# First norm inside the setup, and modulation's weight tiles of 4096 columns with three of them in front of the scan

## Chip, cores and metric

The kernel runs on one core of a Trainium2 chip. The metric is the device time of one execution in microseconds; the kernel before takes 2419.62 us (median of 3 runs, 2417.17 to 2423.88).

## What is computed

Two transformer blocks over 256 tokens of width 1024, in float32. What the change touches is the first block's first norm, its projection and S5 branch, and the second block's modulation, which needs only `c`, `c_ctx` and `ada_w` and is computed early, beside the first block:

```python
h = rms_norm(x, norm_mix_pre[l])                 # y * rsqrt(mean(x*x) + 1e-6) * gain
proj = h @ w_in[l]                               # 1024 x 4096: q, k, v, u, gate_logits
...
lam_bar = exp(lam * dt)                          # S5 branch: 32 groups, 64 complex states each
_, states = associative_scan(combine, (decay, bu), axis=1)
y = einsum('gcp,bsgp->bsgc', c_mat, states).real + d_skip * ug
y = gelu(y); o_ssm = y * sigmoid(y @ w_glu + b_glu)
...
merged = gate_attn * (o_attn @ w_branch_attn[l]) + gate_ssm * (o_ssm @ w_branch_ssm[l])
...
def ada_params(cond, w, b):                      # second block, for c and c_ctx, two layers
    m = silu(cond) @ w + b                       # w: 1024 x 6144
    return split(m, 6)
```

## The kernel before, in words

Activations are kept with features on the partitions: `xT` and `hT` are [128, 8 chunks, 256 tokens]. All weights pass through a ring of four slots of 2 MB (`K.ring`, [128, 4096] each). `K.queue` (116) fixes at build time which weight tile goes to which slot; `K.issue` (138) is the program of SyncE in each stage: it issues the next tiles in this order, and waits before each until the products that read the slot's previous tile are done (`K.done_at`). The queue in order is: 8 tiles of `w_in`, 16 of `ada_w`, `ssm_w_glu` (1 MB), 8 of `ada_w`, `w_branch_attn`, `w_branch_ssm`, `w_out`, and so on. A tile of `ada_w` holds 512 columns of all 1024 rows (`rows_of`), so every partition reads eight runs of 2 KB.

Each stage is a block with one program per engine, and a block begins when all engines have left the one before. The stages here:

- `stage_setup` (203): SyncE loads x, half of the parameter vectors and then issues four tiles; ScalarE issues the other half; TensorE turns x and the parameter rows by transposes, and VectorE copies them to `xT` and `params`.
- `stage_norm` (378): ScalarE squares `xT`, TensorE sums over the partitions with `ones`, ScalarE takes the root, VectorE the reciprocal and `hT = xT * gain * rstd`.
- `linear_stage` (532), the projection: 8 tiles of 4 chunks. `ssm_params` (781) runs beside it: GpSimd loads five small tensors and scales them, and TensorE turns them in `first_turns` (805), between the first and the second tile; VectorE works out the scan's tables.
- `stage_ssm_scan` (989): 16 steps. TensorE makes the drive two steps ahead (`make_drive`), then does one ada tile, then reads out the states (four products at line 1033); VectorE rotates and scans, GpSimd rotates back. ScalarE spreads the decay (1096), and after step 1 does `ada_conditions` (silu of c and c_ctx); TensorE's first ada tile waits for that.
- `stage_glu`, then `stage_stick_breaking` (592): attention in 4 pairs of heads; an ada tile before pairs 0 and 1, one in each pair, two behind the last. `stage_merge` (1128) needs both branch weights.

An ada tile is 8 products of one row chunk against 512 columns (`ada_beside`, 1475). The stationary operand is `c`, [128, 8, 62], zero but for columns 30 and 31; its slice `30 - 2i` puts the two results of tile i into rows 2i and 2i + 1 of a PSUM group of 32. Four groups work side by side, each on two of the eight row chunks. `move` copies this to SBUF and `turn` sums the four parts while turning it.

Of the kernel before, what the change touches and what calls it, by code (L numbers as in the profile page):

```python
# [18 lines left out]
ACT = mybir.ActivationFunctionType  # L19
# [29 lines left out]
ADA_SCAN = 16  # L49
# [153 lines left out]
def stage_setup(K):  # L203
# [25 lines left out]
    turned, moved = K.counter("rows_turned"), K.counter("rows_moved")  # L229
    with K.stage() as st:  # L230
        table = K.sb("param_rows", [P, n_tiles, P], ctx=st)
        x_rows = K.sb("x_rows", [P, TT, D], ctx=st)
        ps = K.ps("setup_ps", [P, 2, 512], st)
        block = st.enter_context(nc.Block())
        n_sync = len(pieces) // 2

        @block.sync
        def _(sp):
            sp.dma_start(x_rows[:, :, :], io["x"][0].rearrange("(a p) d -> p a d", p=P)).then_inc(x_loads.sem, x_loads.tick())
            for t, r, n, a in pieces[:n_sync]:  # L240
                if t == n_tiles - 1:
                    sp.wait_ge(made.sem, made.at(1))
                sp.dma_start(table[r:r + n, t, :], a).then_inc(loads.sem, loads.tick())
            K.issue(sp, 0)

        @block.scalar
        def _(act):
            act.wait_ge(made.sem, made.at(1))
            for t, r, n, a in pieces[n_sync:]:
                act.dma_start(table[r:r + n, t, :], a).then_inc(loads.sem, loads.tick())  # L250

# [18 lines left out]
        @block.tensor  # L270
        def _(pe):
            pe.wait_ge(made.sem, made.at(5))
            pe.wait_ge(x_loads.sem, x_loads.at(1))
            for q in range(quads + -(-n_tiles // 4)):
                if q >= 2:
                    pe.wait_ge(moved.sem, moved.at(q - 1))
                if q == quads:
                    pe.wait_ge(loads.sem, loads.at(len(pieces)))
                n = 4 if q < quads else min(4, n_tiles - 4 * (q - quads))
                for j in range(n):  # L280
                    if q < quads:
                        a, c = divmod(4 * q + j, KC)
                        src = x_rows[:, a, c * P:(c + 1) * P]
                    else:
                        src = table[:, 4 * (q - quads) + j, :]
                    mm = pe.transpose(ps[:, q % 2, j * P:(j + 1) * P], src, K.ident[:, :])
                mm.then_inc(turned.sem, turned.tick())

        @block.vector
        def _(dve):  # L290
            for q in range(quads + -(-n_tiles // 4)):
                dve.wait_ge(turned.sem, turned.at(q + 1))
# [6 lines left out]
                dve.tensor_copy(dst, ps[:, q % 2, 0:n * P].rearrange("p (a n) -> p a n", n=P)).then_inc(moved.sem, moved.tick())  # L299

# [291 lines left out]
def stage_stick_breaking(K, qT, kT, v, oT):  # L592
# [9 lines left out]
    with K.stage() as st:  # L602
# [17 lines left out]
        def _(pe):  # L620
# [33 lines left out]
            for i in range(pairs):  # L654
                sum_later(i)
                if i + 2 < pairs:
                    make_scores(i + 2)
                ada_multiply(pe, i + 2)
                mix(i)
            for n in range(pairs + 2, ada_tiles):  # L660
                ada_multiply(pe, n)
            ada_turn(pe)
# [50 lines left out]
        def _(dve):  # L713
# [33 lines left out]
            ada_move(dve, lambda out, x: dve.tensor_copy(out, x))  # L747
# [241 lines left out]
def stage_ssm_scan(K, S, uT, yT):  # L989
# [4 lines left out]
    with K.stage() as st:  # L994
# [12 lines left out]
        def _(pe):  # L1007
# [10 lines left out]
            make_drive(1)  # L1018
            for i in range(ST):
                if i + 2 < ST:  # L1020
                    make_drive(i + 2)
                if i == 0:
                    pe.wait_ge(silued.sem, silued.at(2))
                    pe.wait_ge(cleared.sem, cleared.at(2))
                ada_multiply(pe, i)
# [10 lines left out]
            ada_turn(pe)  # L1036
# [55 lines left out]
        def _(act):  # L1092
            for i in range(ST):
# [3 lines left out]
                if i == 1:  # L1097
                    ada_conditions(K, None, act)
            ada_move(act, lambda out, x: act.activation(out, x, ACT.Copy))
# [277 lines left out]
def queue_first_block(K):  # L1377
    io = K.io
    queue_columns(K, io["w_in"][0], 4096)
    ada = [(l, c) for l in range(2) for c in range(0, 6 * D, 512)]  # L1380
    for l, c in ada[:ADA_SCAN]:
        K.queue((0, (KC, 512), rows_of(io["ada_w_2"][l], c, 512)))
    queue_columns(K, io["ssm_w_glu"][0], 512)
    for l, c in ada[ADA_SCAN:]:
        K.queue((0, (KC, 512), rows_of(io["ada_w_2"][l], c, 512)))
# [13 lines left out]
def first_block(K):  # L1399
    gain = lambda name: (lambda c: K.col(name, c))  # L1400
    with ExitStack() as K.part:
# [4 lines left out]
        with ExitStack() as banks:  # L1406
            with ExitStack() as ssm:
# [3 lines left out]
                stage_norm(K, K.xT, K.hT, gain("norm_mix_pre"))  # L1411
# [55 lines left out]
def ada_setup(K):  # L1467

    K.ada = {"row": K.sb("ada_row", [P, 512], ctx=K.part), "c": K.sb("ada_c", [P, KC, 62], ctx=K.part),
             "parts": K.sb("ada_parts", [P, 32], ctx=K.part)}


def ada_beside(K, first, n):
# [8 lines left out]
    def multiply(pe, i):  # L1484

        w = K.tile(pe, g0 + i, KC)
        for k in range(2):
            for part in range(4):
                mm = pe.matmul(ps[32 * part:32 * part + 32, :], c[:, 2 * part + k, 30 - 2 * i:62 - 2 * i], w[:, 2 * part + k, :],
                               start=i == 0 and k == 0, stop=i == n - 1 and k == 1, tile_position=(0, 32 * part),  # L1490
                               skip_group_check=True)
        mm.then_inc(full.sem, full.tick())
        K.done_at[g0 + i] = full.count

    def turn(pe):

        pe.wait_ge(free.sem, free.at(1))
        for j in range(4):
            pe.matmul(tiles[:, first:first + n, j, :], row[:, j * P:(j + 1) * P], parts[:, 0:2 * n], start=True, stop=True)

    def move(eng, copy):

        eng.wait_ge(full.sem, K.done_at[g0 + n - 1])
# [1657 lines left out]
```

## Time and profile before

| | us |
|---|---|
| median of 3 runs | 2419.62 |
| the profiled execution's own time | 2414.2 |
| its span | 2412.4 |
| TensorE busy with products | 2161.8 (90%) |
| VectorE, ScalarE, GpSimd busy | 610.2, 440.1, 224.8 |
| DMA | 575.46 MB, 239 GB/s over the span |

Times in the rows are microseconds from the span's start. "PE" is TensorE's products, "PEld" its weight loads, "DVE" VectorE, "ACT" ScalarE, "POOL" GpSimd, "SP" SyncE, and a q behind a name is the engine's queue of issues. A float32 product appears as two records. "idle before <- X" is how long the engine had been idle and whose work ended it. The profile's clock is the share of 2.4 GHz that was granted to TensorE; 0.5 is 1.2 GHz. A stretch's mean lies between.

### The profile page before, as it was taken

How to read it: one execution, taken by the hardware profiler on the slowest of the kernel's cores; microseconds unless marked ns; L12 is line 12 of the kernel's file. 1: busy time of each engine (PE TensorE's matmuls, PEld its weight loads, DVE VectorE, ACT ScalarE, POOL GpSimd, SP SyncE). 2: the span in 40 equal slices, each digit the busy share in tenths (PEclk: the TensorE clock that was granted, in tenths of full speed). 3: DMA queues.
4: the chain of work that ended last, by engine and by line, in shares of the span. 5: the costliest groups of instructions: out<-in, count | busy, mean ns of one | idle time of the engine just before them, and what ended most of it. 6: DMA issues, size and time to landing. Idle time of an engine off the chain costs nothing. (4 is left out here: it accounts for less than half of the span.)

```text
span 2412.4 us, 25196 instructions
## 1 busy us (share of the span) xinstructions
PE 2161.8 (90%) x10420; PEld 1393.5 (58%) x10420; DVE 610.2 (25%) x1387; ACT 440.1 (18%) x835; POOL 224.8 (9%) x352
## 2 busy tenths in 40 slices
PE   6989799779999898889988999898879899988887
PEld 5754486668878755577767433333358754333334
DVE  3557221122210324753223111111012221111111
ACT  1221311112211325533322000000011210000001
POOL 2024100001010114100000100000000000000000
PEclk8999999989999799989888999999989899999998
DMA  6469933224432121210037999999944679999994
GB/s 205 140 224 387 365 140 116 94 87 140 150 137 87 35 70 35 70 36 1 1 119 291 407 428 427 427 427 428 420 172 148 244 326 428 427 428 428 427 428 192
DMA packets 123662, 575.46 MB, mean 239 GB/s; under 512 B 5216, under 2 KB 28345, under 8 KB 99481
## 3 DMA queue, kind: packets, MB, share of 16 engines
q1 hardware_dynamic: 122079, 570.59, 59.5%
q10 hardware_dynamic: 970, 2.23, 0.3%
q8 instruction: 87, 1.43, 0.2%
q0 software_dynamic: 496, 0.97, 0.2%
q14 instruction: 30, 0.25, 0.0%
HBM read 572.72 MB, written 1.05 MB: 238 GB/s over the span
## 5 line engine op out<-in xcount | busy, mean ns | idle before, releaser
L567 PE MATMUL linear_ps<-hT,ring 128*128 128x256 f32 x1216 | 267.2, 382 | 14.4 <-PEq L384 12.4
L2749 PE MATMUL ex_u<-ring_extra,ex_xt 128*64 128x512 f32 x1024 | 235.2, 614 | 36.9 <-DMA ring_extra<-in_w 36.9
L567 PEld LDWEIGHTS linear_ps<-hT,ring 128*128 128x128 f32 x1216 | 232.6, 192 | 48.8 <-issue 16.9
L2749 PE MATMUL ex_u<-ring,ex_xt 128*64 128x512 f32 x1024 | 230.3, 604 | 28.5 <-DMA ring<-in_w 27.0
L2749 PEld LDWEIGHTS ex_u<-ring_extra,ex_xt 128*64 128x64 f32 x1024 | 81.8, 141 | 188.2 <-issue 188.2
L2749 PEld LDWEIGHTS ex_u<-ring,ex_xt 128*64 128x64 f32 x1024 | 81.3, 139 | 173.9 <-issue 173.9
L1831 PE MATMUL dl_front<-dn_src,ring 128*128 128x256 f32 (+1 forms) x512 | 177.5, 503 | 2.4 <-DVE dp_cv L1998 2.4
L2854 DVE TENSOR_TENSOR ex_hid<-ex_sil,ex_u 128x512 f32<-128x512 f32 x32 | 34.8, 1088 | 496.2 <-PE ex_u L2749 496.2
L1279 PE MATMUL ffn_ps<-hT,ring 128*128 128x256 f32 x704 | 154.9, 384 | 5.9 <-PEq L442 5.9
L1279 PEld LDWEIGHTS ffn_ps<-hT,ring 128*128 128x128 f32 x704 | 135.6, 193 | 25.2 <-issue 6.3
L1831 PEld LDWEIGHTS dl_front<-dn_src,ring 128*128 128x128 f32 x512 | 100.0, 200 | 65.6 <-issue 57.9
L2722 PE MATMUL ex_yT<-ex_back,ex_ys 128*128 128x256 f32 x512 | 124.2, 385 | 3.0 <-DVE ex_ys L2865 1.6
L2787 PE MATMUL ex_u<-ring_extra,ex_hidT 128*64 128x512 f32 x512 | 113.8, 596 | 1.0 <-ACT ex_hidT L2811 1.0
L2722 PEld LDWEIGHTS ex_yT<-ex_back,ex_ys 128*128 128x128 f32 x512 | 92.2, 190 | 37.5 <-issue 21.1
L2787 PE MATMUL ex_u<-ring,ex_hidT 128*64 128x512 f32 x512 | 113.4, 595 | 0.0
L2688 POOL COPY ex_xt<-hT 128x256 f32 x60 | 24.1, 402 | 742.2 <-PE ex_u L2749 580.3
L2865 DVE COPY ex_ys<-ex_u 128x512 f32<-128x512 f32 x32 | 22.1, 692 | 239.1 <-PE ex_u L2787 239.1
L1347 PE MATMUL down_ps<-ffn_hid,ring 128*128 128x256 f32 x352 | 78.0, 384 | 4.6 <-PEq L1264 4.6
L2807 ACT ACTIVATE ex_sil<-ex_u 128x512 f32<-128x512 f32 x32 | 19.1, 597 | 318.0 <-PE ex_u L2749 318.0
L1347 PEld LDWEIGHTS down_ps<-ffn_hid,ring 128*128 128x128 f32 x352 | 67.8, 193 | 14.4 <-issue 5.0
L2787 PEld LDWEIGHTS ex_u<-ring_extra,ex_hidT 128*64 128x64 f32 x512 | 35.2, 137 | 69.6 <-issue 68.1
L2787 PEld LDWEIGHTS ex_u<-ring,ex_hidT 128*64 128x64 f32 x512 | 35.3, 137 | 69.3 <-issue 69.3
(549 smaller groups left out, 2511.1 us busy)
## 6 DMA issues: line engine op xcount, KB each, us to landing
ring<-in_w SPq DMA_DIRECT2D x96, 2048.0 KB, 25.3
ring_extra<-in_w SPq DMA_DIRECT2D x92, 2048.0 KB, 25.7
ring<-in_ada_w SPq DMA_DIRECT2D x24, 2048.0 KB, 13.2
ring<-in_ffn_w_up SPq DMA_DIRECT2D x22, 1024.0 KB, 6.5
ring<-in_w_in SPq DMA_DIRECT2D x8, 2048.0 KB, 8.7
ring<-in_w_in_a SPq DMA_DIRECT2D x8, 2048.0 KB, 8.5
ring<-in_w_in_b SPq DMA_DIRECT2D x6, 2048.0 KB, 18.5
ring<-in_ffn_w_down SPq DMA_DIRECT2D x5, 2048.0 KB, 8.1
```

The costliest lines, as they stand in the source:

```text
L567: mm = pe.matmul(ps[:, q % banks, 0:n], w[:, k, j * P:(j + 1) * P], src[:, k, 0:n], start=k == 0, stop=k == kc - 1)
L1279: mm = pe.matmul(ps[:, c % 4, j * T:(j + 1) * T], w[:, j * KC + k, (c % per) * P:(c % per + 1) * P], src[:, k, :], start=k == 0, stop=k == ...
L1347: mm = pe.matmul(ps[:, c // 2, c % 2, :], w[:, f % per, c * P:(c + 1) * P], hid[:, f, :], start=f == 0 and c % 2 == 0, stop=f == FC - 1 an ...
L1831: mm = pe.matmul(ps[:, h % 2, 0:segs * T], w[:, i, (h % 4) * P:(h % 4 + 1) * P], src[:, i, 0:segs * T], start=i == 0, stop=i == KC - 1)
L2688: ins = pool.tensor_copy(xt[:, p % 2, 4 * i:4 * i + 4, H * a:H * a + H], part[:, :, bass.ds(start, H)])
L2722: mm = pe.matmul(yT[:, c // 2, c % 2, :], ys[:, p % 2, c * P:(c + 1) * P], back[:, p % 2, :], start=p == 0 and c % 2 == 0, stop=p == pairs ...
L2749: mm = pe.matmul(u[H * a:H * a + H, i, :], xt[:, b, k, H * a:H * a + H], w[a][:, 512 * k:512 * k + 512], start=k == 0, stop=k == KC - 1, s ...
L2787: mm = pe.matmul(u[H * a:H * a + H, n, :], hidT[:, k, H * a:H * a + H], cols, start=k == 0, stop=k == fc - 1, skip_group_check=True)
L2807: act.activation(sil[:, :], u[:, 0, :], ACT.Silu).then_inc(silued.sem, silued.tick())
L2854: dve.tensor_tensor(hid[:, :].rearrange("s (k q) -> s k q", k=fc), sil[:, :].rearrange("s (q k) -> s k q", k=fc), u[:, 1, :].rearrange("s ...
L2865: dve.tensor_copy(ys[:, p % 2, 512:1024], u[:, 1, :]).then_inc(y1_moved.sem, y1_moved.tick())
```

## The change

Three parts. First, the norm's stage is gone. The setup now squares x while the tokens are on the partitions (ScalarE, the sum over a token's features from the accumulator), takes root and reciprocal on two columns, scales the rows (`n_rows`, half by VectorE, half by ScalarE), turns them by sixteen more transposes, and multiplies by the gain on the way from PSUM to `hT`. SyncE issues two weight tiles in the setup instead of four; the other two go out at the projection's start. Second, an ada tile is now either one row chunk against its first 4096 columns (one run of 16 KB per partition), or, each third, the last 2048 columns of two row chunks (two DMAs with runs of 8 KB). Each layer is 12 tiles as before, but all of a layer has to be there before its results can be moved. Third, 18 instead of 16 tiles are done in the scan's stage, three of them in front of its first step, none in its last; six instead of eight are left for the attention. Layer 0 is moved and turned inside the scan. ScalarE does the conditions before its first spread.

```diff
-ADA_SCAN = 16
+ADA_SCAN = 18
+ADA_FRONT = 3
...
-            K.issue(sp, 0)
+            K.issue(sp, 0, until=2)
+
+        all_moved = TT * KC // 4 + -(-n_tiles // 4)
 
         @block.scalar
         def _(act):
             act.wait_ge(made.sem, made.at(1))
             for t, r, n, a in pieces[n_sync:]:
                 act.dma_start(table[r:r + n, t, :], a).then_inc(loads.sem, loads.tick())
+            act.wait_ge(made.sem, made.at(4))
+            act.activation(root[:, TT:TT + 1], K.epsb[:, :], ACT.Sqrt)
+            act.wait_ge(x_loads.sem, x_loads.at(1))
+            for t in range(TT):
+                act.activation(n_rows[:, t, :], x_rows[:, t, :], ACT.Square, scale=D ** -0.5,
+                               accum_out=root[:, t:t + 1]).then_inc(squared.sem, squared.tick())
+            act.wait_ge(squared.sem, squared.at(TT))
+            act.activation(root[:, 0:TT], root[:, 0:TT], ACT.Sqrt, bias=K.epsb[:, :]).then_inc(rooted.sem, rooted.tick())
+            act.wait_ge(inverted.sem, inverted.at(1))
+            act.activation(n_rows[:, 1, :], x_rows[:, 1, :], ACT.Copy, scale=root[:, 1:2]).then_inc(scaled.sem, scaled.tick())
+            act.wait_ge(moved.sem, moved.at(all_moved))
+            for c in (2, 3, 6, 7):
+                act.wait_ge(chunked.sem, chunked.at(c // 2 + 1))
+                act.activation(K.hT[:, c, :], n_ps[:, c // 2, c % 2, :], ACT.Copy, scale=gain(c))
...
+            pe.wait_ge(scaled.sem, scaled.at(2))
+            for c in range(KC):
+                for t in range(TT):
+                    mm = pe.transpose(n_ps[:, c // 2, c % 2, t * P:(t + 1) * P], n_rows[:, t, c * P:(c + 1) * P], K.ident[:, :])
+                if c % 2:
+                    mm.then_inc(chunked.sem, chunked.tick())
...
+                if q == quads:
+                    dve.wait_ge(rooted.sem, rooted.at(1))
+                    dve.reciprocal(root[:, 0:TT], root[:, 0:TT]).then_inc(inverted.sem, inverted.tick())
+                    dve.wait_ge(inverted.sem, inverted.at(1))
+                    dve.tensor_scalar(n_rows[:, 0, :], x_rows[:, 0, :], root[:, 0:1], None, ALU.mult).then_inc(scaled.sem, scaled.tick())
...
+            dve.wait_ge(moved.sem, moved.at(all_moved))
+            for c in (0, 1, 4, 5):
+                dve.wait_ge(chunked.sem, chunked.at(c // 2 + 1))
+                dve.tensor_scalar(K.hT[:, c, :], n_ps[:, c // 2, c % 2, :], gain(c), None, ALU.mult)
...
-                ada_multiply(pe, i + 2)
+                if i + 2 < ada_tiles:
+                    ada_multiply(pe, i + 2)
                 mix(i)
             for n in range(pairs + 2, ada_tiles):
                 ada_multiply(pe, n)
-            ada_turn(pe)
+            ada_turn(pe, 1)
...
+            pe.wait_ge(silued.sem, silued.at(2))
+            pe.wait_ge(cleared.sem, cleared.at(2))
+            for n in range(ADA_FRONT):
+                ada_multiply(pe, n)
             for i in range(ST):
                 if i + 2 < ST:
                     make_drive(i + 2)
-                if i == 0:
-                    pe.wait_ge(silued.sem, silued.at(2))
-                    pe.wait_ge(cleared.sem, cleared.at(2))
-                ada_multiply(pe, i)
+                if i + ADA_FRONT < ADA_SCAN:
+                    ada_multiply(pe, i + ADA_FRONT)
+                if i + ADA_FRONT == ADA + 1:
+                    ada_turn(pe, 0)
...
+            ada_conditions(K, None, act)
             for i in range(ST):
                 if i >= 2:
                     act.wait_ge(scanned.sem, scanned.at(i - 1))
                 act.activation(rr[:, i % 2, :], S["cos"][:, i, :], ACT.Identity, scale=0.0, bias=S["r"][:, i:i + 1]).then_inc(spread.sem, spread.tick())
-                if i == 1:
-                    ada_conditions(K, None, act)
-            ada_move(act, lambda out, x: act.activation(out, x, ACT.Copy))
+                if i + ADA_FRONT == ADA:
+                    ada_move(act, 0, lambda out, x: act.activation(out, x, ACT.Copy))
...
-                stage_norm(K, K.xT, K.hT, gain("norm_mix_pre"))
...
+def ada_products(t):
+
+
+
+    q, kind = divmod(t, 3)
+    if kind < 2:
+        return [(2 * q + kind, j, 512 * j) for j in range(8)]
+    return [(2 * q + h, 8 + j, 2048 * h + 512 * j) for h in range(2) for j in range(4)]
+
+
+def queue_ada(K, g):
+
+    l, t = divmod(g, ADA)
+    q, kind = divmod(t, 3)
+    w = lambda k, c, n: K.io["ada_w_2"][l, k * P:(k + 1) * P, c:c + n]
+    if kind < 2:
+        K.queue((0, (1, SLOT), w(2 * q + kind, 0, SLOT)))
+    else:
+        K.queue(*((2048 * h, (1, 2048), w(2 * q + h, SLOT, 2048)) for h in range(2)))
...
-        w = K.tile(pe, g0 + i, KC)
-        for k in range(2):
-            for part in range(4):
-                mm = pe.matmul(ps[32 * part:32 * part + 32, :], c[:, 2 * part + k, 30 - 2 * i:62 - 2 * i], w[:, 2 * part + k, :],
-                               start=i == 0 and k == 0, stop=i == n - 1 and k == 1, tile_position=(0, 32 * part),
-                               skip_group_check=True)
+        l, t = divmod(first + i, ADA)
+        g = g0 + i
+        pe.wait_ge(K.landed[K.slot[g]], K.need[g])
+        w = K.ring[K.slot[g]]
+        if l and t == 0:
+            pe.wait_ge(free.sem, free.at(1))
+        for m, (k, j, at) in enumerate(ada_products(t)):
+            part = j % 4
+            mm = pe.matmul(ps[32 * part:32 * part + 32, :], c[:, k, 30 - 2 * j:62 - 2 * j], w[:, at:at + 512],
+                           start=t == 0 and m < 4, stop=t == ADA - 1 and m >= 4, tile_position=(0, 32 * part), skip_group_check=True)
         mm.then_inc(full.sem, full.tick())
-        K.done_at[g0 + i] = full.count
-
-    def turn(pe):
+        K.done_at[g] = full.count
```

## Rows read from the trace of the kernel before

**Rows 1.** Timeline, first 35 us: start, us, engine, line, operation, idle before.

```profile
6.06 3.48 PE L286 MATMUL setup_ps<-ident,x_rows 128*128 128x128 f32 x16 [6.06 <-DMA x_rows<-in_x]
...
7.14 0.27 ACTq L250 DMA_DIRECT2D param_rows<-in_onorm_a  x1
...
12.03 0.91 PE L286 MATMUL setup_ps<-ident,param_rows 128*128 128x128 f32 x5 [2.48 <-DMA param_rows<-in_final_norm]
...
18.71 1.28 ACT L395 ACT_TABLE_LOAD   x1 [18.71 <-PEq L230]
...
20.01 2.00 ACT L395 ACTIVATE hT<-xT 128x1024 f32<-128x1024 f32 x2
...
33.20 15.61 PE L567 MATMUL linear_ps<-hT,ring 128*128 128x256 f32 x64 [5.91 <-PEq L384]
```

**Rows 2.** Timeline of SyncE's queue at 17 to 19 us.

```profile
13.12 5.18 SPq L151 DMA_DIRECT2D ring<-in_w_in  x1
```

**Rows 3.** Timeline of TensorE in the scan.

```profile
150.88 1.92 PE L1489 MATMUL ada_ps<-ring,ada_c 128*32 128x512 f32 x16 [1.42 <-ACT ada_c L1521]
...
156.81 3.62 PE L1033 MATMUL ssm_yp<-ssm_pz,ssm_cT 128*32 128x256 f32 x8 [4.00 <-POOL ssm_pz L1089]
...
170.56 1.89 PE L1033 MATMUL ssm_yp<-ssm_pz,ssm_cT 128*32 128x256 f32 x8
...
175.19 1.89 PE L1033 MATMUL ssm_yp<-ssm_pz,ssm_cT 128*32 128x256 f32 x8
```

**Rows 4.** Stretches: length; PE, PEld, DVE, ACT, POOL busy (count); clock; DMA share; GB/s.

```profile
7.55:14.00 6.45, 2.90 (x16) 1.83 (x14) 3.20 (x6) 0.00 (x0) 0.00 (x0) 0.88 0.95 264
...
14.00:18.70 4.70, 0.00 (x0) 0.00 (x0) 0.00 (x0) 0.00 (x0) 0.00 (x0) 0.50 1.04 383
...
160.00:166.50 6.50, 6.50 (x25) 2.33 (x24) 4.03 (x6) 0.51 (x1) 2.27 (x3) 0.53 0.03 10
...
168.00:222.00 54.00, 54.00 (x331) 22.63 (x331) 51.12 (x72) 5.59 (x11) 29.81 (x22) 1.00 1.05 386
...
287.00:293.10 6.10, 6.09 (x16) 4.96 (x17) 0.00 (x0) 0.00 (x0) 0.00 (x0) 0.56 1.03 392
...
1400.00:1500.00 100.00, 97.94 (x456) 40.94 (x453) 12.37 (x28) 6.57 (x11) 6.01 (x16) 0.98 1.01 427
```

**Rows 5.** Timeline from the scan's end to the merge.

```profile
229.38 1.92 PE L1489 MATMUL ada_ps<-ring,ada_c 128*32 128x512 f32 x16 [1.37 <-DMA ring<-in_ada_w]
...
231.14 1.89 PE L1033 MATMUL ssm_yp<-ssm_pz,ssm_cT 128*32 128x256 f32 x8
...
233.28 1.33 ACT L1102 ACTIVATE ssm_y<-ssm_y 128x256 f32<-128x256 f32 x4
...
243.36 0.71 PE L626 MATMUL sb_z<-proj 64*128 64x256 f32 x4 [1.29 <-PEq L544]
...
276.43 3.64 PE L1489 MATMUL ada_ps<-ring,ada_c 128*32 128x512 f32 x32
...
280.88 1.07 PE L1499 MATMUL ada_t<-ada_parts,ada_row 128*128 128x16 f32 x8 [0.81 <-DVE ada_row L747]
...
287.01 3.75 PE L1147 MATMUL merge_ps<-o_attn,ring 128*128 128x256 f32 x8 [5.06 <-DMA ring<-in_w_branch_ssm]
```

**Rows 6.** Line 1249 (cross attention): the read of an accumulator; ns min/median/max.

```profile
L1249 ACT ACTIVATION_READ_ACCUMULATOR xa_p<-xa_s,xa_nm x8: 192/198/203, 451.0 to 475.0; 128x1 f32 x8
```

**Rows 7.** DMA issues at 7.6 and at 147.5 us: count, KB, us to landing.

```profile
ring<-in_w_in SPq DMA_DIRECT2D x1, 2048.0 KB, 9.0
...
ring<-in_ada_w SPq DMA_DIRECT2D x1, 2048.0 KB, 8.1
```

**Rows 8.** Timeline of the projection's first two tiles.

```profile
42.15 3.65 POOL L874 TENSOR_SCALAR ssm_cx<-ssm_cr,ssm_half 128x256 f32<-128x256 f32 x4
...
48.73 0.23 PE L807 MATMUL ssm_ps<-ident,ssm_ldr 16*128 16x16 f32 x1
...
49.82 13.98 PE L567 MATMUL linear_ps<-hT,ring 128*128 128x256 f32 x64
```

More of the change, by code:

```diff
@@ L229, in stage_setup @@
     turned, moved = K.counter("rows_turned"), K.counter("rows_moved")
+    squared, rooted, inverted, scaled, chunked = (K.counter(n) for n in (
+        "norm_squared", "norm_rooted", "hn_inverted", "norm_scaled", "rt_rowed"))
     with K.stage() as st:
@@ L232, in stage_setup @@
         x_rows = K.sb("x_rows", [P, TT, D], ctx=st)
+        n_rows = K.sb("x_normed", [P, TT, D], ctx=st)
+        root = K.sb("x_root", [P, TT + 1], ctx=st)
         ps = K.ps("setup_ps", [P, 2, 512], st)
+        n_ps = K.ps("setup_normed", [P, KC // 2, 2, T], st)
+        gain = lambda c: K.col("norm_mix_pre", c)
         block = st.enter_context(nc.Block())
@@ L746, in _ @@
                 store(i)
-            ada_move(dve, lambda out, x: dve.tensor_copy(out, x))
+            ada_move(dve, 1, lambda out, x: dve.tensor_copy(out, x))
         @block.sync
@@ L1035, in _ @@
                 mm.then_inc(y_full.sem, y_full.tick())
-            ada_turn(pe)
         @block.vector
@@ L1379, in queue_first_block @@
     queue_columns(K, io["w_in"][0], 4096)
-    ada = [(l, c) for l in range(2) for c in range(0, 6 * D, 512)]
-    for l, c in ada[:ADA_SCAN]:
-        K.queue((0, (KC, 512), rows_of(io["ada_w_2"][l], c, 512)))
+    for g in range(ADA_SCAN):
+        queue_ada(K, g)
     queue_columns(K, io["ssm_w_glu"][0], 512)
-    for l, c in ada[ADA_SCAN:]:
-        K.queue((0, (KC, 512), rows_of(io["ada_w_2"][l], c, 512)))
+    for g in range(ADA_SCAN, 2 * ADA):
+        queue_ada(K, g)
     for n in ("w_branch_attn", "w_branch_ssm"):
@@ L1484, in multiply, with turn, move @@
     def multiply(pe, i):
-        w = K.tile(pe, g0 + i, KC)
-        for k in range(2):
-            for part in range(4):
-                mm = pe.matmul(ps[32 * part:32 * part + 32, :], c[:, 2 * part + k, 30 - 2 * i:62 - 2 * i], w[:, 2 * part + k, :],
-                               start=i == 0 and k == 0, stop=i == n - 1 and k == 1, tile_position=(0, 32 * part),
-                               skip_group_check=True)
+        l, t = divmod(first + i, ADA)
[8 more added lines that the diff above has]
+                           start=t == 0 and m < 4, stop=t == ADA - 1 and m >= 4, tile_position=(0, 32 * part), skip_group_check=True)
         mm.then_inc(full.sem, full.tick())
-        K.done_at[g0 + i] = full.count
-    def turn(pe):
+        K.done_at[g] = full.count
+    def turn(pe, l):
         pe.wait_ge(free.sem, free.at(1))
         for j in range(4):
-            pe.matmul(tiles[:, first:first + n, j, :], row[:, j * P:(j + 1) * P], parts[:, 0:2 * n], start=True, stop=True)
-    def move(eng, copy):
-        eng.wait_ge(full.sem, K.done_at[g0 + n - 1])
+            pe.matmul(tiles[:, ADA * l:ADA * (l + 1), j, :], row[:, j * P:(j + 1) * P], parts[:, 0:2 * ADA], start=True, stop=True)
+    def move(eng, l, copy):
+        eng.wait_ge(full.sem, K.done_at[g0 + ADA * (l + 1) - 1 - first])
         copy(row[:, :], ps[:, :]).then_inc(free.sem, free.tick())
```

## Prediction

> **What bounds the kernel now.** I read three views in this order: the timeline of the first 35 us, the table of stretches, and the timeline from the scan to the merge. In the first 33 us TensorE has almost nothing to do: it turns x and the parameters and is done at 12.94, ScalarE starts the first norm at 18.71, and the first product of the projection starts at 33.20 [rows 1]. Between 13.7 and 18.71 no engine works; SyncE's queue is still inside the fourth 2 MB issue, which ends at 13.12 + 5.18 = 18.30 [rows 2], and the stage can't end before it. The projection then is TensorE's: 13.98 us for each weight tile at full clock, and nothing waits for DMA.
>
> From 148.3, where the projection ends, two things share the bound. In the scan TensorE has a drive product, an ada tile and a read-out per step, and a step takes 175.19 - 170.56 = 4.63 us [rows 3]; the transfers run without a gap at 386 GB/s from 168 to 222 [rows 4], 2.097 MB / 386 = 5.43 us a tile. So the queue is slower than TensorE, and only the three ada tiles that were loaded ahead hide it. The lead runs out at the end of the scan (1.37 us idle for an ada tile), and at 287.01 TensorE has sat 5.06 us for w_branch_ssm [rows 5]. What the queue lost stands in one row: from 160 to 166.5 it moved 10 GB/s while TensorE's clock was 0.53 [rows 4]. All four slots were full, and the step that frees one was slow because TensorE, idle for 4.00 us before 156.81, worked at its lower level of 1.2 GHz. After the merge TensorE is the bound again; each later stage is set by slots that earlier products free, so I let all behind 317.5 move as one piece. This costs nothing in my sum; the price if untrue is in the range.
>
> **Part 1: the norm in the setup.** Removed is everything from 18.71 to 33.20. Added to ScalarE behind its last parameter issue (7.14 + 0.28 = 7.42): a table load 1.28 and a one-column root, some 0.2 (8.90); two squares of 128x1024 at 1.00 with a read of the accumulator at 0.20 each (11.30); a root on two columns and a reciprocal, together about 0.6 with their semaphores (11.9); a copy of 128x1024 at 1.00 (12.9) [rows 1, 6]. VectorE scales the other half at the same time; the trace has no such instruction of that size, so I bound it by ScalarE's 1.00 from both sides, half of it and half as much again: it ends between 12.4 and 13.4. I take 13.0. VectorE's four xT copies are ahead of this and the parameter copies behind; the parameters have landed at 12.03, so TensorE turns them until 12.94 and VectorE's delayed copy is hidden behind TensorE's new turns. If it weren't, it would cost 0.9.
>
> Then sixteen more turns. The first sixteen took 3.48 us at full clock [rows 1]. But in the trace of before the clock is at 0.50 from 14.00 to 18.70 [rows 4], after a stretch in which TensorE had been idle for 2.48 us and then worked for 0.91. The new turns start there, so their bounds are 3.5 and 7.0 us; from 287.0 on, continuous work brought the clock back within 6.1 us [rows 4], so I take 5.2 in the middle: 18.2. The last two chunks are both ScalarE's, some 0.4 each by the linear stage's copies, and a change of block some 0.3: the projection starts at 19.3. Bounds 17.6 and 21.1. Its first weights landed at 7.55 + 9.0 = 16.6 [rows 7], earlier, so nothing waits for them. SyncE issues only two tiles in the setup and is free at 8.6, because the first two issues don't stall; tiles 2 and 3 go out when the projection starts and are needed 28 us later. Gain: 33.20 - 19.3 = 13.9. The first four chunks took 15.61 against 13.98 because of the low clock [rows 1, 8]; half of these 1.6 us may go: gain 0.8 (0 to 1.6).
>
> What moves with it: GpSimd's five SSM loads now start at 19.3, while tiles 1 to 3 are on the queue until 16.6 + 3 x 5.43 = 32.9. Before they had the queue for themselves; GpSimd's scalings ran from 42.15 for 3.65 us to 45.80, and TensorE asked for them at 48.73 [rows 8]. The slack is 2.9 us. If the loads land only with the last tile, at 32.9, GpSimd ends at 36.6 and TensorE, there at 34.8, waits 1.8; with their own packets behind that, 5. They are small and come in between, so I take 0.3 (bounds 0 and 5).
>
> Sum of part 1: 13.9 + 0.8 - 0.3 = 14.4 us. The projection itself is unchanged.
>
> **Part 2: tiles of 4096 columns.** The number of products a tile (8, in four groups side by side) and of bytes is the same, so TensorE's time stays: 1.92 us with the drain [rows 3], some 1.75 to the next product. What changes is the run of bytes: 2 KB per row before, 16 KB or 8 KB after. The experts' weights come in runs of 16 KB, and there the queue moves 427 GB/s, against 386 for ada [rows 4]: 4.91 us a tile. I take 427; bounds 386 and 427 (one in three tiles comes in 8 KB runs). The Trainium skill (DMA: Bandwidth & Descriptors, Specifications) puts line rate at 512 B and more, by which 2 KB rows gain nothing from being longer; the two rows speak against it, and by it the sum would be that of the first rival.
>
> **Part 3: three tiles in front.** Keep the clock of before in mind, with 148.3 as the end of the projection. ScalarE now does the conditions first, so the ada products can start at about 150.3 instead of 150.88 [rows 3]; its two rows for the scan come at 150.7, needed at 152.65, hidden. Three tiles take 5.3 us (155.6), then the third drive, about 1.1 (156.7), for which VectorE waits as long. Then ada tile 3 (landed: 147.5 + 8.1 = 155.6 [rows 7]) until 158.4, and the first read-out at 158.4 instead of 156.81. TensorE no longer sits 4.00 us there, so I keep its clock at full level; then the third read-out comes at 158.4 + 2 x 4.63 = 167.7 instead of 170.56. The slots are free at 152, 154 and 155.6, so the queue never stops: tile n has landed at 150.3 + 4.91 (n - 2), tile 17 at 224.0. TensorE by its own pace would be there at 156.7 + 14 x 4.63 = 221.5, so DMA sets the end: 224.0 + 1.75 + two read-outs of 1.8 = 229.4 against 231.14 + 1.89 = 233.03 before. Step 15 has no ada tile. If the clock did fall once more, TensorE would come 4.8 us late (10 us at about half) and the end only 2.3 late. The ada row's copy and turn move into the middle of the scan, where TensorE's 1.08 us are covered by the same 2.5 us of lead; at the end the table load no longer precedes the four gelus [rows 5], gain 0.7.
>
> Attention then starts at 243.36 - 3.6 - 0.7 = 239.1. Its chain over ScalarE, VectorE and GpSimd is untouched, 33.1 us to the end of the last mix; of the 3.64 us of ada products behind it nothing is left, only the wait for VectorE's copies, 0.81 and 0.4, and the turn 1.07 [rows 5]: 274.5, the merge 0.7 later at 275.2. The queue: tile 17 at 224.0, the glu weights 2.7, six tiles 29.5, two branch tiles 10.6: 266.8, so it is 8 us early and TensorE doesn't wait. Gain 287.01 - 275.2 = 11.8. With no wait before it the merge doesn't begin at the low clock: 6.1 us at 0.56 [rows 4] is 2.7 lost; gain 2.7 (0 to 2.7).
>
> **Sum.** 14.4 + 11.8 + 2.7 = 28.9 us. The profiled execution took 2414.2 with a span of 2412.4, so it would take 2385.3; the median of the runs is 5.4 above it, which gives 2419.6 - 28.9 = 2390.7.
>
> **Rivals.** (a) The queue stays at 386 GB/s. Tile 17 lands at 231.8, the scan ends at 237.2, the merge starts 7.8 later, still not waiting for its weights (277.7): 2398.5. For it: the rate of before is that of the same tensor. Against: the experts' row. (b) TensorE waits in the projection for the SSM loads, 5 us: 2395.7. For it: the queue is full then. Against: 2.9 us of slack and small loads. (c) The setup doesn't shrink as summed, because the turns and what follows run at the low level throughout and the block's end holds on to something not in the trace, the projection at 26: 2397.4. For it: the row at 0.50. Against: SyncE is out of the way. (d) Slower: pieces of 16 KB taken from rows 24 KB apart load badly. The branch weights land at 163.6 + 21 tiles; what part 1 gives is used up at 287.0 + 14.4, that is 6.56 us a tile or 320 GB/s. The lowest rate of a busy queue in the trace is 264 GB/s (7.55 to 14) [rows 4], 7.94 us a tile: 29 us above before, 2448.6. Against it: the experts' pieces have the same size, and nothing in the trace suggests that their distance matters. The Trainium skill (DMA: Bandwidth & Descriptors, Latency and other measured facts) tells of such tiles falling to 207 GB/s at a row distance of a large power of two; no run here shows it, and 24 KB is none.
>
> **How the numbers follow.** Forecast 0.66, (a) 0.13, (b) 0.11, (c) 0.07, (d) 0.03. The forecast's own bounds: turns at full clock and 1.6 in the projection give 2388.1; with the runs' scatter of 2.4 below their median, 2384. Upwards (a), or (b) with a turn at the low clock, reach 2400; both together 2404. Range 2384 to 2403. A measurement here can tell 0.3%, 7.3 us, from no change. All cases but (d) are faster by more, unless (a), (b) and (c) meet: faster 0.94, same 0.03, slower 0.03.
>
> **What would show it.** Step by step: the first product of the projection at 19.3 (18 to 21) and no work idle on SyncE before it; SSM turns without a wait; ada transfers at over 415 GB/s with no hole at the start of the scan; clock 1.0 there; the end of the scan set by the ada tile; no wait at the merge and a full clock in it. The prediction is wrong if the queue is at 386, if the turns or the projection's first tile wait, or if the stages behind 317.5 give back time.

## The result, and the profile after

The kernel after takes 2399.8 us (median of 20 runs, 2390.76 to 2418.84) against 2418.44 (median of 20, 2414.10 to 2423.89) for the kernel before. The ratio is 0.9918, with a 95% interval of 0.9907 to 0.9929: some 20 us or 0.8% faster by the ratio (18.6 us between the medians), where 28.9 were forecast. The predicted 2390.7 lies 9 us under the median. Single profiles of either kernel scatter by several us, so the gains below are told stage by stage, and the second profile of each kernel counts as much as the first.

The profiled execution took 2401.16. The page's head, first part and clock row:

```profile
span 2399.4 us, 25200 instructions
...
PE 2168.0 (90%) x10420; PEld 1398.3 (58%) x10420; DVE 608.4 (25%) x1384; ACT 441.6 (18%) x842; POOL 224.6 (9%) x352
...
PEclk9999999889999899989888999999989899999998
```

TensorE has the same 10420 records of products and is busy 6 us longer than before's 2161.8, so the gain is idle time taken out, and something gave part of it back. The timeline of the first 35 us, which answers [rows 1, 8]:

```profile
12.03 0.74 PE L309 MATMUL setup_ps<-ident,param_rows 128*128 128x128 f32 x5 [2.25 <-DMA param_rows<-in_final_norm]
13.10 3.50 PE L314 MATMUL setup_normed<-ident,x_normed 128*128 128x128 f32 x16 [0.33 <-ACT x_normed L269]
...
17.77 14.05 PE L605 MATMUL linear_ps<-hT,ring 128*128 128x256 f32 x64 [1.17 <-PEq L233]
...
30.05 3.65 POOL L913 TENSOR_SCALAR ssm_cx<-ssm_cr,ssm_half 128x256 f32<-128x256 f32 x4 [3.42 <-DMA ssm_cr<-in_ssm_c_im]
...
33.76 1.09 PE L850 MATMUL ssm_ps<-ident,ssm_cx 128*128 128x128 f32 x8 [1.78 <-POOL ssm_cx L913]
```

The projection starts at 17.77 instead of 33.20, its first tile has no stretch at the low clock, and TensorE then waits 1.78 us for GpSimd, which waited 3.42 for its loads. TensorE in the scan, which answers [rows 3, 5]:

```profile
134.78 5.36 PE L1556 MATMUL ada_ps<-ring,ada_c 128*32 128x512 f32 x48 [0.48 <-ACT ada_c L1587]
...
142.87 1.89 PE L1076 MATMUL ssm_yp<-ssm_pz,ssm_cT 128*32 128x256 f32 x8
...
146.19 1.92 PE L1556 MATMUL ada_ps<-ring,ada_c 128*32 128x512 f32 x16 [0.38 <-DMA ring<-in_ada_w]
...
151.17 1.92 PE L1556 MATMUL ada_ps<-ring,ada_c 128*32 128x512 f32 x16 [0.28 <-DMA ring<-in_ada_w]
...
210.45 1.92 PE L1556 MATMUL ada_ps<-ring,ada_c 128*32 128x512 f32 x16 [1.12 <-DMA ring<-in_ada_w]
212.20 1.89 PE L1076 MATMUL ssm_yp<-ssm_pz,ssm_cT 128*32 128x256 f32 x8
215.81 1.91 PE L1076 MATMUL ssm_yp<-ssm_pz,ssm_cT 128*32 128x256 f32 x8 [1.72 <-POOL ssm_pz L1131]
219.01 7.14 PE L605 MATMUL linear_ps<-ssm_y,ring 128*128 128x256 f32 x32 [1.28 <-PEq L1033]
```

From the second step on ten steps in a row wait a few tenths for an ada tile: 151.17 - 146.19 = 4.98 us for this step and 4.94 in the mean (146.19 to 190.68, nine steps), where before went at 4.63. The three steps behind the turn of the ada row wait for nothing, since this turn gives the queue a microsecond, and the last tile waits 1.12. The last read-out waits not for the queue but for GpSimd. The merge:

```profile
264.80 3.12 PE L1189 MATMUL merge_ps<-o_attn,ring 128*128 128x256 f32 x8 [0.49 <-PEq L640]
267.72 2.46 PE L1189 MATMUL merge_ps<-o_ssm,ring 128*128 128x256 f32 x8
270.02 1.89 PE L1189 MATMUL merge_ps<-o_attn,ring 128*128 128x256 f32 x8
```

The wait of 5.06 us for w_branch_ssm [rows 5] is gone, but the merge still begins at the low clock: 3.12 and 2.46 instead of 1.89. The stretches of after (columns as in [rows 4]) show the queue in the scan, and two falls of the clock:

```profile
136.00:206.00 70.00, 67.40 (x420) 28.21 (x416) 62.18 (x89) 9.26 (x18) 37.45 (x28) 1.00 1.01 423
...
255.20:258.60 3.40, 3.40 (x12) 1.98 (x14) 0.34 (x2) 0.00 (x0) 0.00 (x0) 0.50 1.00 356
265.50:268.90 3.40, 3.40 (x9) 2.69 (x8) 0.00 (x0) 0.00 (x0) 0.00 (x0) 0.51 0.96 342
```

From stage to stage, in us of the two profiles; s is the first product of the scan's drive:

| | before | after | gain | forecast |
|---|---|---|---|---|
| projection starts | 33.20 | 17.77 | 15.4 | 13.9 |
| s | 148.32 | 133.16 | 15.2 | 14.4 |
| last read-out ends, from s | 84.71 | 84.57 | 0.1 | 3.6 |
| attention starts, from s | 95.04 | 94.28 | 0.8 | 4.3 |
| merge starts, from s | 138.70 | 131.64 | 7.1 | 11.8 |
| merge's start to the memory's turns | 31.99 | 31.39 | 0.6 | 2.7 |
| sum to there | 319.00 | 296.19 | 22.8 | 28.9 |
| from there to the end | 2093.40 | 2103.21 | -9.8 | 0 |

So there are three questions: where the scan's 3.6 us went, why the SSM loads were late, and whether the last row is a cost of the change.

### The profile page after: what moved, and what is told of

Its sections match the earlier page's. It is cut to its first block and busy times, and to the rows that moved or that the text cites. A ratio compares the mean times of both kernels' runs of the same rounds, so it can differ in the third digit from the quotient of the medians.

```text
span 2399.4 us, 25200 instructions
## 1 busy us (share of the span) xinstructions
PE 2168.0 (90%) x10420; PEld 1398.3 (58%) x10420; DVE 608.4 (25%) x1384; ACT 441.6 (18%) x842; POOL 224.6 (9%) x352
## 5 line engine op out<-in xcount | busy, mean ns | idle before, releaser
L1389 PEld LDWEIGHTS down_ps<-ffn_hid,ring 128*128 128x128 f32 x352 | 67.8, 193 | 14.4 <-issue 5.0
## 6 DMA issues: line engine op xcount, KB each, us to landing
ring<-in_ada_w SPq DMA_DIRECT2D x16, 2048.0 KB, 15.5
```

The costliest lines, as they stand in the source:

```text
L1389: mm = pe.matmul(ps[:, c // 2, c % 2, :], w[:, f % per, c * P:(c + 1) * P], hid[:, f, :], start=f == 0 and c % 2 == 0, stop=f == FC - 1 an ...
```

## The experiments

Times of scan and attention below are counted from s of each kernel.

**One part at a time.** The first three do the new setup alone (the tiles, the scan and the attention are those of before), the new tiles alone (`ADA_SCAN = 16`, `ADA_FRONT = 0`), and three tiles in front alone (`ADA_FRONT = 3`, tiles of 512 columns). The fourth moves the SSM turns behind the projection's second weight tile:

```diff
-    return {1: first_turns, 4: turn_b}, {2: angles, 5: sines, 7: cosines}, programs
+    return {2: first_turns, 4: turn_b}, {3: angles, 5: sines, 7: cosines}, programs
```

> Part 1 alone on the kernel before: norm in the setup, two tiles issued there; ada tiles of 512 columns, none in front. If the parts add up: the projection starts at 17.8 instead of 33.2, its first tile takes 14.0 instead of 15.6, TensorE waits some 1.8 us for the SSM loads, the projection ends 15.2 earlier, and all behind keeps it: 15 us less than before, 2403 us. Rival (parts don't add, since the queue, which bounds the stretch to the merge, doesn't gain from an earlier start): the queue is idle in the projection, so I expect nothing lost; if it were, the wait for w_branch_ssm would grow beyond 5.06 us.

> Part 2 alone on the kernel before: tiles of 4096 columns, 16 in the scan, none in front, conditions after step 1 as before. Theory Q (the queue's rate is worth what I said): the hole of 160 to 166.5 us stays, but the transfers behind run at 427 instead of 386 GB/s, so the two waits at the end of the scan (1.4 and 0.6 us) and the 5.06 us before the merge go, with the low clock behind it: 6 to 9 us less than before, 2410 us. Theory T (the tail of the scan is VectorE's and GpSimd's): the scan's end moves by 1.3 us at most, all else comes at the merge: 5 to 8 us less. They differ in where: Q moves the last read-out by 1.9 us, T by 1.3 or less.

> Three tiles in front alone on the kernel before: tiles of 512 columns, 16 in the scan, conditions first. The queue has no hole, the clock doesn't fall at 156 us. Theory Q: the queue at 5.43 us a tile from tile 4 on: tile 15 lands at 150.3 + 13 x 5.43 = 220.9, steps 13 to 15 have no tile, the last read-out ends at about 230.5, 2.5 earlier than before. Theory T (from the drive of step 15 to the last read-out a chain of 11 us over VectorE and GpSimd): step 13 begins at about 224.5, the chain ends at 236: nothing gained or 3 us lost in the scan. At the merge both have the queue 7 us ahead, so its wait goes: Q 7 to 9 us less than before (2411), T 2 to 5 less (2415).

> The changed kernel with the turns of the SSM tensors behind the second tile of the projection instead of the first, and the angles one tile later. If the 1.85 us that TensorE loses between its first and second tile is a wait for GpSimd's loads, late because tiles 1 to 3 share the queue with them, it goes: 1.8 us less than the changed kernel, about 2398. If the loads aren't the cause but the turns themselves (they need 1.1 us of TensorE anyway), nothing changes. Risk: VectorE's chain of 13 us now ends closer to the turns before the fifth tile; there are 12 us of cover.

Measured, beside 2420.05 for before on that chip:

| | time | ratio (95%) | s | last drive | read-outs end | merge (absolute) |
|---|---|---|---|---|---|---|
| setup alone | 2402.83 | 0.9917 (0.9887 to 0.9947) | 133.63 | 69.17 | 83.80 | 270.10 |
| tiles alone | 2416.05 | 0.9970 (0.9947 to 0.9992) | 149.28 | 67.25 | 80.38 | 281.50 |
| front alone | 2423.55 | 1.0002 (0.9981 to 1.0024) | 148.65 | 77.35 | 90.51 | 291.28 |
| after, later turns | 2395.15 | 0.9880 (0.9848 to 0.9912) | 133.27 | 71.34 | 84.43 | 263.26 |

By the whole time the setup alone can't be told from the kernel after; up to the merge it has 16.9 of the 22.2 us (287.01 - 270.10, against 287.01 - 264.80). The front alone isn't faster than before. Two of these runs missed what was expected. The new tiles alone were to take 2410 and took 2416: the wait for w_branch_ssm at the merge didn't go (1.85 us), because this load was issued only at 272.40, when its slot came free. The front alone was to save 2 to 9 us and ended the scan 5.8 us later than before, against both theories, and waited 2.15 at the merge. The new tiles with nothing in front end the scan 4.2 us before the kernel after does. These two kernels differ in the scan by two tiles more, three in front, and the order on ScalarE; which of it costs the 4.2 us is asked below. The front on the old tiles shows the queue at its worst; its timeline in the scan:

```profile
195.38 1.92 PE L1491 MATMUL ada_ps<-ring,ada_c 128*32 128x512 f32 x16 [0.71 <-DMA ring<-in_ada_w]
...
200.80 1.92 PE L1491 MATMUL ada_ps<-ring,ada_c 128*32 128x512 f32 x16 [0.71 <-DMA ring<-in_ada_w]
```

A step takes 5.42 us with runs of 2 KB, what the prediction worked out from 386 GB/s (5.43), and some 4.94 with the new ones. In a kernel without a DMA wait at the end (tiles alone; the one with half of the bytes below does the same), the last read-out ends 13.1 us after the last drive starts (67.25 to 80.38): this is the chain over VectorE's scan and GpSimd's rotation. With the tiles alone an ada tile stands in the last step too and doesn't lengthen it. In the kernel after it is also 13.1 (71.47 to 84.57), though its last tile waited 1.12 us. So in the kernel after the last tile isn't what ends the scan; the last drive is, and what delays it is the pace of the steps.

With the later turns TensorE doesn't wait for GpSimd, yet s stays at 133.27: in that run the projection's products began 0.43 us apart until 21.5 and 0.22 from then on, so the first 3.6 us of the projection ran at the low level.

**What sets the pace.** Above, Q was a statement on the last tile's arrival; below, the letter stands for one on every step's pace. Two tiles in front instead of three, and, separately, half of the bytes:

```diff
-ADA_FRONT = 3
+ADA_FRONT = 2
```

```diff
-        K.queue((0, (1, SLOT), w(2 * q + kind, 0, SLOT)))
+        K.queue((0, (1, SLOT // 2), w(2 * q + kind, 0, SLOT // 2)))
...
-            mm = pe.matmul(ps[...], c[...], w[:, at:at + 512],
+            mm = pe.matmul(ps[...], c[...], w[:, at % 2048:at % 2048 + 512],
```

> The kernel after, with two ada tiles in front of the scan instead of three, and one in every step (18 in the stage as before; the last step now has one). Theory Q: the third tile in front makes each later tile due one step earlier, so the ring's lead is used up at step 1 and each step of the scan goes at the queue's pace of 4.94 us. With two in front, tile n is due at about 8 + 4.63 x (n - 2) from the start of the scan's drive and lands at 3.1 + 4.94 n, which is late by at most some tenths until tile 15; the waits for DMA in the steps go, the last drive stands at 67 to 68.5 instead of 71.5, the last read-out ends at 80.5 to 82 instead of 84.6, and the time is 2.5 to 4 us below the kernel after. Rival R, the conditions and the steps' other work set the pace and the waits only show it: last drive at 71 to 72, the same time as the kernel after within 1 us. A second rival: the tile of the last step stands in the chain VectorE, GpSimd, TensorE of the last read-outs and takes 1.7 us of it back.

> The kernel after, with half of the bytes of each ada tile not loaded: its products read the first half twice, so modulation's result is another, and TensorE's work is unchanged. It tells the queue from TensorE, VectorE and GpSimd as what sets the scan's pace. Theory Q: a tile lands every 2.5 us, no step waits for DMA, the last drive stands at 67 to 68 from the scan's start instead of 71.5, and the last read-out ends 13.1 later, at 80 to 81 instead of 84.6. Rival: VectorE's and GpSimd's rotation sets the pace, the last drive stays at 71 to 72 and the read-out at 84 to 85. If the front itself (three tiles with no drive beside them) costs time, it shows as a last drive above 67.3, which is what the kernel with nothing in front has.

Beside 2419.85 for before on this chip, two in front take 2395.40 us, ratio 0.9904 (0.9888 to 0.9921), last drive at 67.24, read-outs end at 81.32. Its timeline:

```profile
147.60 1.89 PE L1076 MATMUL ssm_yp<-ssm_pz,ssm_cT 128*32 128x256 f32 x8
...
152.23 1.89 PE L1076 MATMUL ssm_yp<-ssm_pz,ssm_cT 128*32 128x256 f32 x8
156.87 1.89 PE L1076 MATMUL ssm_yp<-ssm_pz,ssm_cT 128*32 128x256 f32 x8
...
212.10 1.92 PE L1556 MATMUL ada_ps<-ring,ada_c 128*32 128x512 f32 x16 [1.09 <-DMA ring<-in_ada_w]
```

The steps are back at 4.63 us, and only the last two tiles wait. Of the 4.2 us that the last drive gains, the tile in the last step takes 1.0 back (14.1 us to the end instead of 13.1), less than the 1.7 of the second rival, and by landing late: it starts at 212.10 behind a wait of 1.09, and the last read-out follows it directly. The scan ends 3.2 us earlier; the whole time isn't shown to be better than that of the kernel after, which didn't run on this chip and had ratios of 0.9918 and 0.9900 on others. With half of the bytes (a ring slot's second half isn't loaded, so modulation's result is another, and the stages behind it go another way; its 4431 us say nothing) the scan's stretch reads:

```profile
165.00:200.00 35.00, 35.00 (x213) 15.34 (x216) 32.82 (x46) 3.93 (x8) 20.45 (x16) 1.00 0.65 224
```

TensorE is busy for all 35 us, and every step but the one with the ada row's turn (5.73) goes at 4.62 to 4.66. Its last drive stands at 69.88, not at 67 to 68, since the scan began at the low clock (its first read-out at 11.40 instead of 9.71, 1.7 late); without that it would be 68.2, an estimate. So the queue's bytes set the pace of the kernel after; VectorE's and GpSimd's rotation doesn't. They are worth 71.5 - 68.2 = 3.3 us of the 4.2; the other 1.0 is the third tile itself, which stands ahead of the last drive also when nothing waits.

**The SSM loads.** SyncE waits for them at the projection's start before it issues weight tiles 2 and 3:

```diff
         @block.sync
         def _(sp):
+            if getattr(K, "hold", None):
+                sp.wait_ge(*K.hold)
+                K.hold = None
             K.issue(sp, g0 + tiles)
...
     loads = K.counter("ssm_loads", 16)
+    K.hold = (loads.sem, loads.at(5))
```

> The kernel after, with SyncE waiting at the projection's start for GpSimd's five small SSM loads before it issues weight tiles 2 and 3. Theory C: these loads landed only at 29.9 because they share the queue with tiles 1 to 3; with tiles 2 and 3 held back they land with tile 1, at 24 or before, GpSimd's scaling is done by 28, TensorE's turns begin behind the second weight tile's end of 31.8 without the wait of 1.8 us, and the scan starts 1.5 to 1.9 earlier, at 131.3 to 131.7. Rival: the loads take 7 us of their own whatever is beside them; then nothing moves, and the scan starts at 133.2. Against theory C too: if tile 2 now comes late (it is needed at about 46), a wait shows behind the second tile's products.

> Both edits together, two ada tiles in front and the SSM loads ahead of weight tiles 2 and 3. If theories Q and C hold, their gains add: 2.5 to 4 us in the scan and 1.5 to 1.9 in the projection, some 4 to 6 us below the kernel after (2395 +- 2 where that took 2399.8), and a ratio to the kernel before of 0.989 to 0.991. If only one holds, 0.990 to 0.9915. If the time gained is taken back by waits for the later weight tiles, which now are asked for earlier, the ratio stays at 0.992, and a DMA wait shows at the merge.

The DMA issues of `ssm_c_im` (count, KB, us to landing), first in the kernel after, then with the hold:

```profile
ssm_cr<-in_ssm_c_im POOLq DMA_DIRECT2D x1, 128.0 KB, 7.8
```

```profile
ssm_cr<-in_ssm_c_im POOLq DMA_DIRECT2D x1, 128.0 KB, 3.6
```

Before, with the queue to itself, the same load took 3.2, and the other three of its size 3.6 to 4.1. The timeline of TensorE with the hold:

```profile
31.46 0.23 PE L850 MATMUL ssm_ps<-ident,ssm_ldr 16*128 16x16 f32 x1
31.62 1.09 PE L854 MATMUL ssm_ps<-ident,ssm_cx 128*128 128x128 f32 x8
```

No wait, and s at 131.02, 2.1 earlier (1.8 of it behind the projection's start). No later weight tile was late. The whole, a single run, took 2394.17. The wait's size is not a constant: the kernel after again waited 0.98 us, and the one with two tiles in front, whose projection is the same, 3.19, since its last SSM load took 9.2 us to land. Both edits together: 2393.23 us, ratio 0.9888 (0.9872 to 0.9905); s at 130.93, read-outs end at 81.05, merge at 257.49 instead of 264.80. Up to there the gains add; 1.5 of the 7.3 us is a fall of the clock in attention that the kernel after had in its first profile and not in its second.

**The stalled queue.** Four tiles issued in the setup, as before, with the new norm (`until=4` for `until=2`):

> The kernel after, with SyncE issuing four weight tiles in the setup as before, not two. It tells how much of the setup's gain is the removed norm and how much the queue's stall. Theory S, the prediction's: the fourth issue holds SyncE until some 18.3, the block can't end before it, and the projection starts at 18.8 to 19.3 instead of 17.7. Rival: the block's end is set by the new turns alone, SyncE's issue is over by then, and the projection starts at 17.7 as before this edit. The SSM loads land late either way (29 to 31) with a wait of 1.5 to 3.5 us at the turns.

2400.32 us. SyncE's issues and TensorE's first product:

```profile
8.63 9.81 SPq L152 DMA_DIRECT2D ring<-in_w_in  x2
```

```profile
18.88 5.38 PE L605 MATMUL linear_ps<-hT,ring 128*128 128x256 f32 x16 [2.31 <-PEq L233]
```

The last issue ends at 8.63 + 9.81 = 18.44, and the projection follows at 18.88: the stall would have held the block's end 1.1 us longer than the turns do. The SSM turns waited for nothing here, against what was expected, because the projection's first tile took 15.67 us (clock low from 19.7 to 23.1).

**Is the end slower?** Both kernels once more, unchanged, and the one with both edits:

> The kernel after once more, unchanged, for a second profile and for the comparison with the two edits on one chip. If what lies behind the memory turns (2103.2 us in its first profile, 2093.4 in before's) is scatter of TensorE's clock, it comes out anywhere from 2094 to 2104, and goes with the time spent at the low clock (241.6 against 210.7 us). If the change has a lasting cost there, it is at 2103 again. The front up to the merge should repeat within 1.5 us; median 2398 to 2401.

> The kernel before once more, unchanged, for a second profile. Scatter theory: its stretch behind the memory turns, 2093.4 in the first profile, was a low draw (that profile lies 4 to 5 us under the median of before), and comes out at 2096 to 2102 now. If the change has a lasting cost there, it is at 2093 to 2094 again. The front (projection at 33.2, merge at 287) should repeat within 1.5 us.

> Two ada tiles in front and the SSM loads ahead of weight tiles 2 and 3, once more, beside the kernel after on one chip. From the stages up to the merge it should be 7 us faster than the kernel after (merge at 257.5 against 264.8); of this, 1.3 to 2 us was the clock's fall in attention, which may come or not. So 5 to 7 us below the kernel after in the medians, ratio to before 0.9885 to 0.9900. If the gain is given back behind the merge, under 3 us.

On one chip with before at 2420.47: after 2395.77 (ratio 0.9900, 0.9875 to 0.9925), both edits 2392.81 (0.9880, 0.9855 to 0.9905), before's own second profile 2422.03. The stretch from the memory's turns to the end (length; TensorE busy and products; clock; DMA share; GB/s), for before, before again, after, after again:

```profile
319.00:2412.40 2093.40, 1890.61 (x9038) 0.95 0.59 237
```

```profile
315.05:2420.30 2105.25, 1907.61 (x9038) 0.94 0.58 235
```

```profile
296.19:2399.40 2103.21, 1903.33 (x9038) 0.94 0.58 236
```

```profile
295.31:2390.80 2095.49, 1898.60 (x9038) 0.95 0.59 237
```

The same 9038 records of products take 2093 and 2105 us in two executions of the kernel before, and 2103 and 2095 in two of after. Each goes with the time at the low clock between that point and the span's end (208.6, 249.0, 239.5, 225.9 us). Over the thirteen profiles with the same work there, the stretch is some 0.31 us longer for each us at the low clock, with a correlation of 0.92. So the 9.8 us "given back" in the first pair of profiles is within the scatter between executions of one kernel (12 and 8 us), and the second pair has 9.8 of the other sign. That the clock is its cause rests on this correlation, and a lasting cost of 2 or 3 us isn't excluded.

Up to the merge the kernel after repeats (264.80 and 264.22), while before came 2.7 us earlier than in its first profile (287.01 and 284.30), more than the 1.5 expected. Most of it is before's scan, 82.15 from s instead of 84.71: the clock was low there for 6.8 us instead of 10.3. So in the second pair the change gives 14.4 us up to s, and its scan is 2.2 us longer than before's, not 0.1 shorter; up to the memory's turns it gives 19.8 instead of 22.8.

That both edits beat the kernel after is plain up to the merge (258.08 against 264.22). Over the whole execution the medians differ by 3.0 us on this chip, where 5 to 7 were expected, with intervals that overlap.

## Why the prediction was right, and where not

**Right in sign, kind and range.** No rival came true as a case, though (b) did in part. The queue went at 423 to 428 GB/s in the scan with rows 24 KB apart, so (a) and (d) fall; the projection started before 19.3, so (c) does.

**The new turns: their price was the low one already.** The prediction took 5.2 us from bounds of 3.5 "at full clock" and 7.0; they took 3.50. The step that failed is the reading of [rows 1]: the first sixteen turns' 3.48 us were not at full clock. The stretches of after, then of before, then of after again (length; TensorE busy and count; clock; DMA share; GB/s):

```profile
12.00:12.80 0.80, 0.74 (x5) 1.00 1.04 407
13.10:16.30 3.20, 3.20 (x15) 0.50 1.05 394
```

```profile
6.00:9.00 3.00, 2.94 (x13) 1.00 0.68 64
9.05:9.40 0.35, 0.35 (x4) 1.00 1.00 138
```

```profile
18.16:21.28 3.12, 3.12 (x8) 1.00 1.05 385
21.28:24.40 3.12, 3.12 (x16) 1.00 1.03 376
```

At 0.50 a turn takes 3.20/15 = 0.21 us. At the start of before the turns also begin 0.21 apart, and from 9.05 on 0.11, though both stretches read 1.00. The last pair tells why: a record of the same product takes 3.12/8 = 0.39 us and then 3.12/16 = 0.195 under the same reading, since this trace's first clock record is at 21.3, and what lies before the first record is shown as 1.00 whatever it was. In before the first record is at 9.0. So the full-clock price of sixteen turns is about 1.7 us (an estimate, 16 x 0.11), 3.5 is the low one, and the start ran at the low level. The Trainium skill (TensorE: Matmul & The Clock Gate, Part 4: PE-mode transpose) has the full clock not come on for transposes. The traces here have it both ways: in before it rose behind nothing but turns, at 9.05, and in after again it stayed low through all 37 turns of the setup and rose at 21.3, 3.1 us into the projection. With the right price the projection's start was 17.6, which is what came. The scaled rows (13.0 forecast, 13.1 measured) were right. That part 1's sum comes so close (14.4 forecast, 15.2 measured) is in part luck: the start came 1.5 us earlier and the first tile gained 1.6 instead of 0.8, and the SSM wait took 1.5 of it back. The first tile's gain isn't certain either: in after again, with the later turns and with four tiles issued, it began or fell to the low level and took 15.5 to 15.7 us.

**The SSM wait, 0.3 against 1.78.** The mechanism was named as rival (b); its size was taken near the wrong bound. "They are small and come in between" fails: beside weight tiles they took 7.8 us to land instead of 3.6.

**The scan, 3.6 against 0.1.** Two terms failed. The sum said that the queue only sets the end, at tile 17, and that TensorE by its own pace is 2.5 us ahead. But tile n is due three steps earlier than before. By the forecast's own formula (tile n landed at 150.3 + 4.91 (n - 2), TensorE there at 156.7 + 4.63 (n - 3)) the queue is behind from tile 9 on; in the trace it is from tile 4 on, which TensorE wanted at 12.65 from s and which landed at 13.0 (forecast 11.8: issued at 136.77, it took 9.4 us, with the next tile's parts on the queue beside it). From there ten drives, and not only the last tile, go at the queue's 4.94, and tile 17 was used at 77.3 (forecast 75.7): 1.2 from tile 4's landing, the rest from the pace. Then "1.75 + two read-outs of 1.8" leaves out the chain of VectorE and GpSimd: 7.3 us instead of 5.4. The two errors, 1.6 and 1.9, make the 3.5 us. Set against before's second profile, whose scan was 2.6 us shorter, the scan lost 2.2 us instead of gaining 3.6. The table load (0.6 of 0.7) was right.

**Attention and merge.** The merge has no DMA wait, as forecast, and it was right that the queue is well ahead. But attention took 1.5 us longer from a fall of the clock at 255.2 to 258.6 that the second profile doesn't have (33.17 against 34.66 to the last mix). And "with no wait before it the merge doesn't begin at the low clock" is wrong: the clock fell at the merge in every profile but that of the front on the old tiles, the kernel after with its 0.49 us of wait among them. Before that point TensorE mostly waits in attention's chain. Of 2.7 us, 0.6 came in the first pair and none in the second (30.76 before, 31.09 after).

**The base.** The argument from one profiled execution carried more scatter than the forecast's terms: before's second profile lies 8 us above its first. The miss of 9.1 us against the median is 6.1 up to the memory's turns (the scan and the stage behind it 3.6, the merge 2.1, attention 1.2, less the 0.8 that part 1 did better) and 3.0 behind them: of the 9.8 there, 5.4 and 1.4 fall away when each profile is set against its median.

## What to carry to other kernels

Loading ahead is only worth something as a lead: work put in front of a loop makes every later transfer due that many steps earlier, and where the queue is slower than the loop by a few per cent, the loop takes on the queue's pace from its first steps. Leave as many tiles in front as the lead covers; here two did all but at the loop's end, and three didn't. Small loads that a stage needs should be issued, and have landed, before large transfers are put beside them. And before pricing a cost by a duration, make sure at which clock it was measured: two instructions of the same shape far apart in time tell more than a mean over a stretch without records.

## What was not expected of the hardware

- Products at the very start ran at the low level in all fourteen profiles here, and the view's clock is no evidence ahead of its first record (9.0 to 24.3 us into the span in the profiles here).
- Five loads of 128 KB or less, issued beside weight tiles of 2 MB, landed in 6.1 to 8.0 us (one took 9.2 in the kernel with two tiles in front), instead of 1.9 to 4.1 before and 3.6 to 4.6 with the hold.
- The clock's falls come and go between executions of the same kernel: 3.4 us at the scan's start in two of the nine profiles with new tiles and a front (1.7 us lost), in attention in the kernel after's first profile and not in its second (1.5 us lost), and in the long stretch behind the merge, which took 2093 and 2105 us in the kernel before.
